# A transformer layer with 32 experts on one core: the up projection of the next expert goes in front of the down projection of this one, and the weight loads follow that order

## The reference, cut to what matters

```
logits = xt @ w_router + b_router
top_val, top_idx = lax.top_k(logits, TOP_K)            # 4 of 32
combine = one_hot(top_idx) weighted by softmax(top_val)
for e in range(32):
    hid = clamped_swiglu(xt @ w_mlp1[e] + b_mlp1[e])     # 1024 -> 2048 -> 1024
    y = y + combine[:, e:e+1] * (hid @ w_mlp2[e] + b_mlp2[e])
return layer_norm(ALPHA * h + y)                       # ln3
```

## Time and profile before

| | |
|---|---|
| time, median of 3 runs | 1174.39 us |
| the profiled execution's own time | 1173.93 us |
| its span | 1172.2 us |
| PE busy | 1080.3 us (92%) |
| DVE busy | 321.4 us (27%) |
| ACT busy | 256.9 us (22%) |
| read from HBM | 444.16 MB, 380 GB/s over the span |
| chain that ended last | PE 56%, DMA 27%, SP's queue 10%, ACT 3%, DVE 2% |

### The profile page before, as it was taken

How to read it: one execution, slowest core, us unless ns; L and a number is a source line. 1 busy time by engine, 2 the same in 40 slices (tenths; PEclk the granted TensorE clock), 3 DMA queues, 4 the chain that set the end, 5 groups by cost and what they waited for, 6 DMA issues and landing times.

```text
span 1172.2 us, 16086 instructions
## 1 busy us (share of the span) xinstructions
PE 1080.3 (92%) x6592; PEld 521.4 (44%) x6593; DVE 321.4 (27%) x727; ACT 256.9 (22%) x421; POOL 9.1 (1%) x14
## 2 busy tenths in 40 slices
PE   7999999999999999999999888888888888888995
PEld 5787799863333333333333333333333333333331
DVE  4986785461112111111111111111111111111114
ACT  3575655431111111111111111111111111111100
POOL 0000000000000000000000000000000000000000
PEclk9999999979999999999999999999999999999997
DMA  8756677499999999999999999999999999999993
GB/s 294 270 180 225 215 268 259 179 369 410 430 427 427 428 429 428 429 429 428 428 428 428 428 429 428 429 429 429 428 429 428 428 428 429 428 429 429 426 411 133
DMA packets 49597, 445.64 MB, mean 380 GB/s; under 512 B 5536, under 2 KB 6176, under 8 KB 24896
## 3 DMA queue, kind: packets, MB, share of 16 engines
q1 hardware_dynamic: 49568, 445.23, 92.0%
HBM read 444.16 MB, written 1.05 MB: 380 GB/s over the span
## 4 chain that ended last, share of the span: by engine, by line
PE 56%; DMA 27%; SPq 10%; ACT 3%; DVE 2%; issue 1%; POOL 0%; DVEq 0%; ACTq 0%
DMA ring<-in_w_mlp 25%; PE bank L937 21%; PE bank L970 12%; SPq L437 8%; PE bank L551 4%; PE bank L553 4%; PE bank L552 4%; PE bank L865 3%; PE bank L856 2%; DMA w_raw<-in_w_in 2%; ACT live L1228 1%; ACT live L1204 1%; PE bank L923 1%; PE bank L766 1%; PE bank L812 1%
## 5 line engine op out<-in xcount | busy, mean ns | idle before, releaser
L937 PE MATMUL bank<-ring,live 128*64 128x512 f32 x2048 | 457.3, 597 | 38.3 <-DMA ring<-in_w_mlp 38.3
L937 PEld LDWEIGHTS bank<-ring,live 128*64 128x64 f32 x2048 | 142.5, 137 | 332.2 <-issue 248.1
L970 PE MATMUL bank<-ring,live 128*64 128x512 f32 x1024 | 230.2, 603 | 22.0 <-ACT live L1228 22.0
L1641 DVE TENSOR_SCALAR live<-bank 128x256 f32<-128x256 f32 x64 | 24.2, 419 | 745.8 <-PE bank L937 745.8
L970 PEld LDWEIGHTS bank<-ring,live 128*64 128x64 f32 x1024 | 71.5, 138 | 158.6 <-issue 130.5
L1224 ACT ACTIVATE live<-live 128x512 f32<-128x512 f32 x32 | 20.1, 629 | 464.8 <-DVE live L1641 464.8
L1269 DVE TENSOR_TENSOR w_low<-w_raw,w_high 128x1024 fp32r<-128x1024 f32 x64 | 75.2, 1219 | 25.7 <-ACT w_high L1034 25.1
L1034 ACT ACTIVATE w_high<-w_raw 128x1024 fp32r<-128x1024 f32 x64 | 65.4, 1059 | 36.7 <-DMA w_raw<-in_w_in 17.0
L1230 ACT ACTIVATE live<-bank 128x512 f32<-128x512 f32 x32 | 19.1, 598 | 233.4 <-PE bank L970 233.4
L551 PE MATMUL bank<-w_high,left 128*128 128x512 f32 x160 | 64.1, 401 | 5.5 <-DVE w_low L1269 3.9
L865 PE MATMUL bank<-live 64*128 64x512 f32 x256 | 63.6, 615 | 0.7 <-ACT live L1230 0.7
(11 more groups left out here) (197 smaller groups left out, 788.6 us busy)
## 6 DMA issues: line engine op xcount, KB each, us to landing
ring<-in_w_mlp SPq DMA_DIRECT2D x192, 2048.0 KB, 48.1
w_raw<-in_w_in SPq DMA_DIRECT2D x24, 512.0 KB, 8.7
w_raw<-in_w_mem_kv SPq DMA_DIRECT2D x16, 512.0 KB, 3.9
w_raw<-in_w_mix_out SPq DMA_DIRECT2D x8, 512.0 KB, 4.8
w_raw<-in_w_mem_q SPq DMA_DIRECT2D x8, 512.0 KB, 3.8
w_raw<-in_w_mem_o SPq DMA_DIRECT2D x8, 512.0 KB, 4.2
h<-in_x SPq DMA_DIRECT2D x4, 256.0 KB, 4.8
mem_o<-in_mem SPq DMA_DIRECT2D x2, 512.0 KB, 8.7
```

Source lines behind the costliest of these rows:

```text
L937: mm = pe.matmul(up[n][64 * g:64 * g + SLOTS, :], x_e[:, k, :], slot(at)[:, col:col + 512], start=False, stop=(k == KC - 1))
L970: mm = pe.matmul(ty[64 * g:64 * g + SLOTS, :], hidT[:, P * c + 64 * u:P * c + 64 * u + SLOTS], slot(at)[:, D * c + 512 * g:D * c + 512 * ( ...
```

## The change

The order on PE in the loop was U(n), D(n), U(n+1), D(n+1); it becomes U(n+1), D(n), U(n+2), D(n+1). The scatter of the expert two before goes behind the first piece of the up projection, the transposes of hidden values and picks behind its second piece. The loads go in the same order. The last expert has tensors of its own (`last_hidT`, `last_y`, `last_back`) and result banks of its own, so that D30 and D31 can follow each other, and the last piece, D31.1, comes in two halves with a semaphore each. `hidT` no longer shares memory with `lin`; `sig` shares it with `y_e`. The loops for the first and for further sweeps become one, whose count comes from a second value, `more` (sweeps less one). The load of `b2` now stands behind the loop over all experts' loads.

The loads (SP):

```diff
-            load_expert(2, 0, 0)
-            load_expert(3, 1, 1)
-            with sp.Fori(1, E // 2 - 2) as i:
+            load_up(2, 0, 0)
+            load_up(3, 1, 1)
+            load_down(2, 0, 0)
+            with sp.Fori(0, E // 2 - 2) as i:
                 for parity in range(2):
-                    load_expert(sp.snap(2 * i + parity + 2), sp.snap(2 * i + parity), parity)
-            load_expert(E - 2, E - 4, 0)
-            wait_piece_used(E - 2, 0)
-            sp.dma_start(b2[:, :], a["b_mlp2"][0]).then_inc(b2_in, 16)
-            load_expert(E - 1, E - 3, 1)
+                    load_up(sp.snap(2 * i + parity + 4), sp.snap(2 * i + parity + 2), parity)
+                    load_down(sp.snap(2 * i + parity + 3), sp.snap(2 * i + parity + 1), 1 - parity)
...
+            sp.wait_ge(up_used, sp.snap(more * (E * (UP_PIECES - 1)) + ((E - 2) * (UP_PIECES - 1) + 1)))
+            sp.dma_start(b2[:, :], a["b_mlp2"][0]).then_inc(b2_in, 16)
+            sp.wait_ge(down_used, sp.snap(more * E + (E - 2)))
+            load(E - 1, UP_PIECES, PIECES + UP_PIECES)
+            sp.wait_ge(down_done, sp.snap(more * E + (E - 2)))
+            for i, landed in enumerate((half_in, piece_in[NSLOT - 1])):
+                half_piece = slice(2 * D * i, 2 * D * (i + 1))
+                sp.dma_start(slot(NSLOT - 1)[:, half_piece], expert_src(E - 1, PIECES - 1)[:, half_piece]).then_inc(landed, 16)
```

PE, inside the up projection (`up_stage`) after chunk k (two chunks are a piece):

```diff
                     if k % 2:
-                        mm.then_inc(pieces_used if k < KC - 1 else up_done, 1)
+                        mm.then_inc(up_used if k < KC - 1 else up_done, 1)
+                    if k == 1 and earlier is not None:
+                        two_ago, one_ago = earlier
+                        if two_ago is not None:
+                            pe.wait_ge(y_ready, two_ago)
+                            pe.wait_ge(back_ready, one_ago)
+                            scatter(first=first_sum)
+                    if k == 1 and ending:
+                        turn_weights()
+                    if k == 3 and ending:
+                        pe.wait_ge(wtT_ready, 1)
+                    if k == 3 and earlier is not None:
+                        turn_hidden(one_ago, ty)
+                        turn_picks(one_ago)
...
-                    if ending and k == 3:
-                        add_down_bias(0)
-                    if ending and k == 5:
-                        add_down_bias(1).then_inc(bias_added, 1)
+                    if ending and k in (3, 5):
+                        add_down_bias(k // 4)
```

PE, the order of the loop and the end (n counts experts from 1 here):

```diff
+            with pe.Fori(0, pe.snap(more * (E // 2) + (E // 2 - 3))) as i:
                 for parity in range(2):
...
+                    up_stage(n, ups[parity], pe.snap(16 * i + 48), earlier=(two_ago, one_ago))
+                    gather_next(n)
+                    down_stage(one_ago, downs[1 - parity], pe.snap(16 * i + (48 if parity else 32)), ty)
...
+            up_stage(of_end[1], ups[0], loads, earlier=(of_end[3], of_end[2]), tokens=True)
+            gather_next(of_end[1])
+            down_stage(of_end[2], downs[1], pe.snap(more * (8 * E) + (8 * E - 16)), ty)
+            up_stage(of_end[0], ups[1], loads, earlier=(of_end[2], of_end[1]), ending=True)
+            pe.wait_ge(back_ready, of_end[0])
+            turn_picks(of_end[0])
+            down_stage(of_end[1], downs[0], loads, ty, between=lambda: turn_hidden(of_end[0], up[0]))
...
+            down_stage(of_end[0], downs[1], loads, up[1], between=scatter_before, halves=True)
+            pe.wait_ge(y_ready, of_end[0])
+            pe.wait_ge(back_ready, pe.snap(more * E + (E + 1)))
+            scatter(last=True)
```

More of the change, by code:

```diff
@@ L858, in gather, with scatter @@
                 mm.then_inc(gathered, 1)
-            def scatter(last, first=False):
+            def scatter(first=False, last=False):
+                weights, rows_out = (last_back, last_y) if last else (back, y_e)
                 for t in range(NT):
                     for g in range(2):
+                        if first:
+                            bank_for(pe, "Y", t, g)
                         rows = slice(64 * g, 64 * g + SLOTS)
-                        mm = pe.matmul(acc[t][g][:, :], back[rows, t, :], y_e[rows, :], start=first, stop=last)
+                        mm = pe.matmul(acc[t][g][:, :], weights[rows, t, :], rows_out[rows, :], start=first, stop=last)
                         if last:
                             mm.then_inc(all_added, 1)
-                if not last:
-                    mm.then_inc(scattered, 1)
             def add_tokens(part):
@@ L891, in add_down_bias, with turn_picks @@
                 return mm
[L893 to L898, removed]
+            def turn_picks(n):
+                pe.wait_ge(pick_w_ready, n)
                 for t in range(NT):
-                    mm = pe.transpose(ty[:, P * t:P * (t + 1)], pick_w[:, t, :], ident)
+                    mm = pe.transpose(xg[:, P * t:P * (t + 1)], pick_w[:, t, :], ident)
@@ L901, in exchange, with turn_hidden @@
                 mm.then_inc(turned, 1)
[L902 to L920, removed]
+            def turn_hidden(n, to):
+                pe.wait_ge(hid_ready, n)
+                for q in range(4):
+                    mm = pe.transpose(to[:, P * q:P * (q + 1)], glu[:, q:512:4], ident)
+                mm.then_inc(hid_turned, 1)
@@ L921, in serve, with up_stage @@
+            def up_stage(n, at, loads, earlier=None, first=False, first_sum=False, tokens=False, ending=False):
+                pe.wait_ge(hot_ready, n)
+                pe.wait_ge(up_read, n)
+                for j in range(2):
                     for g in range(2):
-                        col = 1024 * g + 512 * n
-                        mm = pe.matmul(up[n][64 * g:64 * g + SLOTS, :], hot[:, :], bias_parts[:, col:col + 512],
+                        col = 1024 * g + 512 * j
+                        mm = pe.matmul(up[j][64 * g:64 * g + SLOTS, :], hot[:, :], bias_parts[:, col:col + 512],
@@ L930, in serve @@
                     if k % 2 == 0:
-                        at = piece(k // 2)
+                        pe.wait_ge(piece_in[at + k // 2], loads)
                     if first and k == 4:
                         pe.wait_ge(x_e_ready, 1)
-                    for n in range(2):
+                    for j in range(2):
                         for g in range(2):
-                            col = 2048 * (k % 2) + 1024 * g + 512 * n
-                            mm = pe.matmul(up[n][64 * g:64 * g + SLOTS, :], x_e[:, k, :],
-                                           slot(at)[:, col:col + 512], start=False, stop=(k == KC - 1))
+                            col = 2048 * (k % 2) + 1024 * g + 512 * j
+                            mm = pe.matmul(up[j][64 * g:64 * g + SLOTS, :], x_e[:, k, :],
+                                           slot(at + k // 2)[:, col:col + 512], start=False, stop=(k == KC - 1))
@@ L959, in serve, with gather_next @@
[L959 to L965, removed]
+                    if ending and k in (3, 5):
+                        add_down_bias(k // 4)
+            def gather_next(n):
+                pe.wait_ge(pick_ready, n)
+                pe.wait_ge(back_ready, n)
+                gather()
@@ L966, in serve, with down_stage @@
+            def down_stage(n, at, loads, to, between=None, halves=False):
+                pe.wait_ge(hidT_ready, n)
+                stationary = last_hidT if halves else hidT
                 for u in range(2):
-                    at = piece(UP_PIECES + u)
+                    if halves and u == 1:
+                        pe.wait_ge(half_in, 16)
+                    else:
+                        pe.wait_ge(piece_in[at + u], loads)
                     for c in range(4):
+                        if halves and u == 1 and c == 2:
+                            pe.wait_ge(piece_in[at + u], loads)
@@ L985, in _ @@
-            with pe.Fori(1, E // 2 - 1) as i:
-                for parity in range(2):
[L987 to L994, removed]
-                    with pe.Fori(0, E // 2) as i:
-                        for parity in range(2):
-                            before = pe.snap(s * E + 2 * i + parity)
-                            serve(pe.snap(before + 1), before,
-                                  piece_of(parity, pe.snap(s * (8 * E) + 16 * i + 16)))
@@ L1000, in _ @@
-            served = pe.snap(sweeps * E)
-            pe.wait_ge(y_ready, served)
-            pe.wait_ge(back_ready, served)
-            scatter(True)
+                    mm.then_inc(down_done if u else down_used, 1)
+                    if u == 0 and between:
+                        between()
+            ups, downs = [PIECES * parity for parity in range(2)], [PIECES * parity + UP_PIECES for parity in range(2)]
+            up_stage(1, ups[0], 16, first=True)
+            for t in range(NT):
+                pe.wait_ge(part_ready[t], 3)
@@ new lines, in _ @@
+            gather_next(1)
```

(45 more changed lines are left out.)

127 lines of the change are left out of this document (49 added, 78 removed).

## The result

| | median | runs |
|---|---|---|
| kernel before, beside it | 1175.22 us | 4, 1174.37 to 1176.55 |
| changed kernel | 1188.62 us | 4, 1188.27 to 1189.49 |

The change makes the kernel slower: the ratio is 1.0114, with a 95% interval of 1.0101 to 1.0127. That is 13.4 us. The direction and the main mechanism, PE's wait for `b2`, are those of the prediction, but it gave 9.8 us, and the time lies 0.6 us above the end of its range.

A forecast was written before the change was run, and what follows sets the result against it. DMA was taken to bound the kernel. D31's end at 1138.5 (`b2` landing, with -1.1 at the start) + 28.3 (remaining PE work) + 1.7 (clock) = 1168.5 against 1158.66 made +9.8, median 1184.2 us; range 1181 to 1188.

The forecast's parts named there:

- PE's wait for `b2`: Near the end, after U31.1: PE stands at `b2_in` from about 1122 for 16 us; the wait as forecast had chance 0.83.
- What bounds the kernel: Expert loop: DMA binds at 29.39 us an expert, against 25.8 us of PE work in the new order.
- PE's saved copies and new waits: Loop on PE: two ACT copies, 0.60 + 0.57 us, leave the chain; worth nothing as long as DMA binds.
- The place of `b2`: Load queue at the loop's end: `b2`, issued behind D30.1 with 11 pieces ahead, lands four pieces later than before.
- some 51: Load of `b2`: some 51 us from issue to landing, in place of 21.1.
- The landing itself: Load of `b2`: lands at 1138.5, from 1120.0 plus four pieces of 4.90 less 1.1 us.
- The rule against it: Load of `b2`: by the skill's completion rule a small transfer may finish before a large one ahead, so `b2` could be early.
- the cost of the clock behind the wait: After PE's idle for `b2`: PE comes back at the lower clock, costing 1.7 us; bounds 0 and 3.6.
- The start of the loop: Loop start, 280 to 290 us: the DMA hole of 382 GB/s closes, -1.1 us; bounds 0 and -3.7.
- The sum: End of kernel: D31 ends at 1168.5 against 1158.66; span +9.8, profiled execution 1183.7, median 1184.2 us.
- The first rival: Tail: `b2` is there in time, PE only follows DMA, D31 ends at 1152.4; 1168.2 us; chance 0.10.
- PE as the bound of the loop: Expert loop: waits at nearly every piece drop the clock, costing 1.5 us an expert; about 1214 us; chance 0.03.

The follow-up runs named there:

- the first trace: Changed kernel as it stands, the run traced for the result, against the kernel before: 1188.62 us, ratio 1.0114.
- second trace of the changed kernel: Changed kernel run again unchanged, to look at the stages ahead of the experts, against the kernel before: 1188.01 us, ratio 1.0107.
- third trace: Changed kernel run again unchanged, beside the run with 32 extra matmuls, against the kernel before: 1188.43 us, ratio 1.0103.

## Why the prediction was right in kind and short in size

**What bounds the kernel.** Right. 428 GB/s in both stretches, 29.37 us an expert, PE's saved copies and new waits without effect.

**The place of `b2`.** Right, and shown from both sides: moved to the front again in the new order the loss is gone (1170.75), moved forward by two pieces three quarters of it are gone (1178.46), made in the old order it appears (1193.29), and with the readers moved behind it it is gone too (1171.12). The wait of "16 us" measured 15.6, 15.75 and 15.73 in three traces, and `b2` took 47.2 to 47.3 us to land ("some 51"). That is shorter because the issue came late, 5.8 us after U30.0 was used up, while SP was still issuing the pieces in front. The landing itself came 1.6 to 3.6 us later than reckoned; that is taken up below.

**The rule against it.** The Trainium skill, DMA: Bandwidth & Descriptors, section Queues, rings and completion order, has each DMA engine take descriptors in ring order, and allows a small transfer on few engines to complete ahead of a large one. In none of the eight traces where it stood far back did `b2` do so: 42.5 us with nine pieces still to land at its issue, 47.2 to 49.2 with ten. The traces agree with the rule on ring order; its exception isn't seen for this load.

**The step that failed: the cost of the clock behind the wait.** "I take 1.7. Bounds: 0, and 3.6 if ..." Behind the wait, the four matmuls and U31.2 should take 1.91 + 3.58 = 5.5 us; they took 8.6, 9.2 and 10.2 in the three traces of the changed kernel, 3.1, 3.7 and 4.7 too much. The prediction sized this by U0 and D31, of which D31 began at full clock and ran at half only from 1150.2 to 1153.6. Behind 15.7 us of idle it was at half from the first matmul and rose only after more than 6 us (still 0.50 in 1147 to 1148 in the first trace). So the term was 1.4, 2.0 and 3.0 us short in the three traces, and in two of them even its upper bound was too low. In the run that was traced for the result it is 1.4; there the landing was the larger miss.

**The start of the loop and the landing: a second step that failed.** The prediction took 1.1 us off for the hole in the DMA rate early in the loop. The hole did close: all ten traces of the new order have 427 to 431 GB/s from 280 to 300 us, and of the three of the old order two have it (404 and 403) and one has 428. In the second trace of the changed kernel, where U0 begins as it did in the trace that the prediction read (256.08 against 255.68), the same bytes have landed at 1107.82 (D29.1) in place of 1108.49 (U30.3), so 0.7 us of the 1.1 are there. But U31.0 then landed 6.1 us behind D29.1 and not 4.9. In the seven traces with `b2` behind U31 this distance is 5.6 to 6.4 us, in the old order it is 4.9 at the same place; the prediction had no term for it, and its cause is open. So `b2` landed at 1140.06 and not at 1138.5. In the first and third trace, where U0 begins 3.2 to 3.3 us later, it landed at 1141.94 and 1142.11, another 1.9 and 2.1 us later.

**The sum, trace by trace.** The prediction gave 1183.7 for a traced run. With the measured landing and clock the first trace comes to 1183.7 + 3.4 + 1.4 = 1188.5 (measured 1188.69), the second to 1183.7 + 1.6 + 2.0 = 1187.3 (1187.40), the third to 1183.7 + 3.6 + 3.0 = 1190.3 (1190.48). So these two terms are the whole miss there. For the medians the base counts too: the runs of the kernel before lie between 1172.07 and 1177.62 with medians of 1175.1 to 1176.4, and the three that the prediction had gave 1174.39, 0.8 less than the four beside the result.

**The first rival (1168.2 us).** With the wait gone the kernel gives 1170.75. It is nearly what the rival said, PE following DMA, only with later bytes: in its trace D31.0 lands at 1145.73 in place of 1143.4, and D31 ends at 1155.05, 9.3 us behind that, where the rival had 3.55 + 1.92 + 3.55 = 9.0. From U31.0 (1116.39) on PE works for 38.7 us without a wait, but this work is just as long as the landings leave it: made shorter at its start it brought a wait for D31.0 and no gain (1170.80). **PE as the bound of the loop:** not seen; the waits of about 1 us left the clock at 1.00.

So the gain of the new order was real: with `b2` in front D31 ends 4.4 us behind the last landing, where it ended 9.6 us behind it (1158.66 - 1149.11), and the median is 4.4 us lower. The load of one small tensor turned this into a loss of 13.4. The best kernels measured here are those without the wait, 1170.8 to 1171.1 us, and between them no difference shows.

## What to carry to other kernels

In a full queue the place of a load is its time of arrival: count the bytes ahead of it, 4.9 us for each 2 MiB here, and compare with the first reader, for small loads above all. When loads are put in a new order, the ones that are issued once, outside the loop, must be placed anew with them. A long wait on PE costs its own length and then the slow clock behind it: here 3 to 5 us more behind waits of 5.7 to 15.7 us, and nothing seen behind waits of about 1 us. In this loop, which DMA bounds, a change of the order on PE paid only at its two ends.

## What the hardware showed that I had not expected

The clock came back after a different time in each trace. Behind a wait of 15.6 to 15.75 us the two groups cost 3.1, 3.7 and 4.7 us extra; behind one of only 5.74 us the cost was 3.1 us as well, and behind one of 14.16 us it was 4.3. In the stages ahead of the experts the clock dropped to 0.75 or 0.83 in the same two places (50 to 60 and 130 to 140 us) in some traces, in one place or in none in others, with the same code, and moved the start of U0 between 255.65 and 259.70 us. The landing of `b2` moved by 1.9 us between the changed kernel's traces with U0 at 256.08 and at 259.35. Their spans are 1185.6 and 1186.9, only 1.3 us apart, since the clock behind the wait cost 0.6 us less in the later one. One trace of a kernel carries this: compare start times of two kernels only with that in mind.

A matmul of 64 stationary columns and 256 moving columns (L963) took 217 ns an instruction (27.84 us for 128), no less than one of 512 moving columns in the projections (3.65 us for 16). Those stand in pairs that write the lower and the upper 64 rows of a bank, the added ones don't. That the pairs run side by side would account for it; no run here took them apart.
